# A two-model transformer kernel: the second layer's projection slabs moved into its attention, and TensorE's step reordered

## What is computed

```python
proj = h @ w_in_b[li]
q, k, v, qm = jnp.split(proj, [qw, 2 * qw, 3 * qw], axis=-1)
y_tok = neighbourhood_attn(q.reshape(B, S, N_Q_HEADS, HEAD_DIM),
                           k.reshape(B, S, N_Q_HEADS, HEAD_DIM),
                           v.reshape(B, S, N_Q_HEADS, HEAD_DIM), rpb_b[li])
y_mem = memory_attn(qm.reshape(B, S, N_MEM_HEADS, HEAD_DIM), mk, mv)
x = x + jnp.concatenate([y_tok, y_mem], axis=-1) @ w_out[i]
```

## Time and profile before

| | |
|---|---|
| median of 3 runs | 2664.66 us (2661.65 to 2667.18) |
| profiled execution, its own time | 2679.11 us |
| its span, first to last instruction | 2677.3 us |
| mean granted TensorE clock | 0.967 |
| busy: PE, PEld, DVE, ACT, POOL | 96%, 83%, 36%, 35%, 45% |

### The profile page before, as it was taken

One profiled execution on the slowest core, in us unless ns is written; L12 is line 12 of the kernel. 1 busy time (PEld: TensorE's weight loads), 2 busy tenths in 40 slices (PEclk: granted clock), 3 DMA queues, 4 the chain that ended last, 5 costly groups with the idle time before them and its releaser, 6 DMA issues.

```text
span 2677.3 us, 47067 instructions
## 1 busy us (share of the span) xinstructions
PE 2569.1 (96%) x16758; PEld 2217.9 (83%) x16758; DVE 959.8 (36%) x1740; ACT 923.9 (35%) x2020; POOL 1201.4 (45%) x1039
## 2 busy tenths in 40 slices
PE   7999999999988999999998879999999989999999
PEld 7767888888866888888997769999999767998897
DVE  4263221223255321226753434422433442442341
ACT  4284322232254322234342223222333663322221
POOL 4554444444483444444442534444444442444443
PEclk9999999999988999999998989999999996999999
DMA  5211232232210222232221002222222000222222
GB/s 172 79 42 63 94 101 87 94 100 88 89 42 25 94 97 92 94 103 90 83 74 40 2 25 87 94 95 86 86 95 71 25 25 24 94 91 97 86 100 96
DMA packets 59469, 209.10 MB, mean 78 GB/s; under 512 B 8544, under 2 KB 11232, under 8 KB 59360
## 3 DMA queue, kind: packets, MB, share of 16 engines
q1 hardware_dynamic: 59360, 207.66, 23.1%
HBM read 205.54 MB, written 2.10 MB: 78 GB/s over the span
## 4 chain that ended last, share of the span: by engine, by line
PE 70%; issue 15%; POOL 8%; DVE 4%; ACT 2%; POOLq 0%; DMA 0%; DVEq 0%; SPq 0%; ACTq 0%
PE ps L1307 57%; POOL w_lo L612 7%; PE ps L1495 2%; PE ps L1477 1%; PE ps L1604 1%; PE ps L1454 1%; PE ps L1426 1%; PE ps L1593 1%; DVE s_sb L1784 1%; PE ps L1439 1%; PE ps L1322 1%; PE ps L1500 1%; DVE y_sb L1759 0%; POOL bias_sb L702 0%; PE ps L1504 0%
## 5 line engine op out<-in xcount | busy, mean ns | idle before, releaser
L612 POOL TENSOR_TENSOR w_lo<-raw,w_hi 128x512 fp32r<-128x512 f32 (+1 forms) x704 | 977.2, 1409 | 1164.3 <-ACT w_hi L863 1163.9
L863 ACT ACTIVATE w_hi<-raw 128x512 fp32r<-128x512 f32 (+1 forms) x704 | 427.2, 653 | 1342.2 <-PE ps L1307 1324.7
L1307 PE MATMUL ps<-h_hi,w_hi 128*128 128x512 f32 (+2 forms) x2992 | 854.3, 332 | 14.6 <-POOL h_lo L789 8.0
L1307 PE MATMUL ps<-h_lo,w_hi 128*128 128x512 f32 (+2 forms) x2992 | 852.7, 332 | 0.0
L1307 PE MATMUL ps<-h_hi,w_lo 128*128 128x512 f32 (+2 forms) x2992 | 850.6, 331 | 0.0
L1307 PEld LDWEIGHTS ps<-h_hi,w_hi 128*128 128x128 f32 x2992 | 510.6, 189 | 75.7 <-issue 17.2
L1307 PEld LDWEIGHTS ps<-h_lo,w_hi 128*128 128x128 f32 x2992 | 506.4, 189 | 55.1 <-issue 1.0
L1307 PEld LDWEIGHTS ps<-h_hi,w_lo 128*128 128x128 f32 x2992 | 507.1, 189 | 54.2
L1307 PE MATMUL ps<-act_lo,w_hi 128*128 128x512 f32 (+1 forms) x880 | 280.5, 351 | 0.0
L1307 PE MATMUL ps<-act_hi,w_lo 128*128 128x512 f32 (+1 forms) x880 | 279.8, 350 | 0.0
L1307 PE MATMUL ps<-act_hi,w_hi 128*128 128x512 f32 (+1 forms) x880 | 278.8, 349 | 0.0
(11 more groups left out here) (264 smaller groups left out, 2539.1 us busy)
## 6 DMA issues: line engine op xcount, KB each, us to landing
raw<-slabs_d SPq DMA_DIRECT2D x288, 512.0 KB, 3.2
raw<-slabs_d SPq DMA_DIRECT2D x64, 704.0 KB, 4.0
bias_sb<-alibi_d SPq DMA_DIRECT2D x6, 384.0 KB, 3.7
x<-x_d SPq DMA_DIRECT2D x1, 2048.0 KB, 13.4
out_d<-x SPq DMA_DIRECT2D x8, 256.0 KB, 4.3
rpb_raw<-rpb_d SPq DMA_DIRECT2D x6, 256.0 KB, 2.7
mem_in<-mem_d SPq DMA_DIRECT2D x1, 1024.0 KB, 9.1
cst<-consts_d SPq DMA_DIRECT2D x1, 792.0 KB, 11.2
```

Of the source, the lines that this page charges most:

```text
L612: nc.gpsimd.tensor_tensor(w_lo[:, s, a * P:b * P], raw[:, s, a * P:b * P], w_hi[:, s, a * P:b * P].bitcast(f32), ALU.subtract).then_inc(lo ...
L863: nc.scalar.activation(w_hi[:, s, a * P:b * P], raw[:, s, a * P:b * P], ACT.Copy)\
L1307: last = nc.tensor.matmul(ps[:, s * 2 * BANK + po:s * 2 * BANK + po + n], w[:, s, wk], a[:, k, to:to + n], start=(k == 0 and w is w_hi and ...
```

## The change

The projection keeps 8 slabs ahead of the attention, the 6 of values and the 2 of memory queries. The other 12, now in the order query tile, key tile, query tile and so on, stand inside the attention. Both attentions are one row of 32 pairs, written out without a loop, with the memory heads' 8 pairs first (`woven_row`). TensorE's step is now the transposes of pair p - 2, the scores of p, the values of p - 3, and then half a slab (12 matmuls of 512 columns) in each of the first 24 pairs. In the last 8 pairs stand pieces of the output projection's first two slabs instead, 3 or 6 matmuls each (`OUT_PARTS`), and the rest of these two slabs follows the last pair. ACT's and POOL's steps take a half slab's rounding and remainder each, DVE's odd steps take a slab out. The projected tiles go through a ring of four (`ring`), staged by POOL four pairs ahead of use; scores go through three banks (1, 3 and 5), and both heads' transposes through bank 4, copied out by one ACT instruction instead of two. The attention's results have buffers of their own (`yw_hi`, `yw_lo`), and SP's loads of slabs and of the bias alternate by tile. The number of slabs, pairs and matmuls is the same.

```diff
-    proj(14, 6, 1)
-    out[-1].queries = (0, 1, 2, 6)
-    out[-1].by_cols = True
+    proj(2, 6, 1)
+    out[-1].queries = (0,)
+    out[-1].by_cols = out[-1].woven = True
+    att(nt=2, blocks=m_blocks, bias=None, sink=None, qt=0, kt=0, group=1, y=6, layer=1)
+    out[-1].woven = True
+    slabs(2 * 2, UP)
     att(nt=6, blocks=n_blocks, bias="rpb", sink=None, qt=0, kt=6, group=1, y=0, layer=1)
-    out[-1].by_cols = True
-    att(nt=2, blocks=m_blocks, bias=None, sink=None, qt=12, kt=0, group=1, y=6, layer=1)
-    tail(4, 1, 1, False, (6, 2, True))
+    out[-1].by_cols = out[-1].woven = True
+    slabs(2 * 4, UP)
+    tail(4, 1, 1, False, (6, 2, True), woven=True)
...
+            def attend_woven(a):
+
+                b = stages[stages.index(a) + 1]
+                first, row = a.slab0 // 2, woven_row(a)
+                chores = {a: prepare(a), b: prepare(b)}
+                for s in range(RING):
+                    pool.wait_ge(acc_free[s], first)
+                for n in (0, 1, 2):
+                    chores[a][n](0)
+                stream(a.slab0 + 2)
+                pool.wait_ge(val_kept, a.val0)
+                for p in row:
+                    u, n = p.at // 4, p.at % 4
+                    if p.at + 4 < len(row):
+                        then = row[p.at + 4]
+                        if then.st is b and n < 2:
+                            pool.wait_ge(acc_free[n], first + then.tile + 1)
+                        chores[then.st][n](then.tile)
+                    if n < 2 and 1 <= u <= W_TILES:
+                        split_lo(first + u, 1, UP, (n,))
+                    if n >= 2 and u < W_TILES:
+                        split_lo(first + u + 1, 0, UP, (n - 2,))
+                    if p.back(3).exists:
+                        y_lo_of(p.back(3).st, p.back(3).tile, p.back(3).b)
...
+                if st.woven:
+                    row = woven_row(st)
+                    for p in row:
+                        probs(p, 0)
+                        if p.back(1).exists:
+                            turned_woven(p.back(1))
+                        probs(p, 1)
+                        if p.back(3).exists:
+                            y_hi(p.back(3))
+                        split_woven(p)
...
+                def out_parts(parts):
+                    q = st.slab0 // 2 + W_TILES
+                    near = stages[stages.index(st) + 1]
+                    for s, k in parts:
+                        if k == DT - 2:
+                            begin(q, s)
+                            second_half(q, s)
+                        pe.wait_ge(y_lo_ready, near.pair0 + 4 * (k + 1) if k < near.nt else st.pair0 + 4 * (k - near.nt + 1))
+                        products(q, s, [k], *outputs(st), DT - 2, near.nt - 1)
...
+                if st.woven:
+                    pe.wait_ge(val_kept, st.val0)
+                    row = woven_row(st)
+                    for p in row:
+                        if p.back(2).exists:
+                            transpose(p.back(2))
+                        scores(p)
+                        if p.back(3).exists:
+                            values(p.back(3))
+                        woven_part(p)
+                    last = row[-1]
+                    transpose(last.back(1))
+                    values(last.back(2))
+                    transpose(last)
+                    out_parts([(1, 3)])
+                    values(last.back(1))
+                    values(last)
+                    out_parts([(0, 4), (1, 4), (0, 5), (1, 5)])
+                    return
...
+                def evict_woven(p):
+                    u, n = p.at // 4, p.at % 4
+                    if u >= W_TILES or n % 2 == 0:
+                        return
+                    s, near = n // 2, stages[stages.index(st) + 1]
+                    ended(st.slab0 // 2 + u, s)
+                    if u >= 1:
+                        wait(qk_staged, near.tile0 + u - 1 if u >= 2 else near.tile0)
+                    to = in_cols(ring_tiles(st, u)[s])
+                    stt(to, in_rows(acc(s, 1)), 1.0 if s else HD ** -0.5, in_rows(rstd[:, SEQ_T]), ALU.mult, ALU.mult)\
+                        .then_inc(acc_free[s], 1)
+                if st.woven:
+                    row = woven_row(st)
+                    for p in row:
+                        scores(p)
+                        evict_woven(p)
+                        if p.back(3).exists:
+                            normalise(p.back(3))
```

257 lines of the change are left out of this document (203 added, 54 removed).

## The result

The changed kernel takes 2652.03 us, the median of 7 runs (2647.65 to 2653.77). The kernel before, with four more runs beside it, takes 2677.51 us (7 runs, 2661.65 to 2681.2). The ratio is 0.9913, with a 95% interval of 0.9888 to 0.9938: faster by 0.9%, about 23 us (the medians are 25.5 us apart). Against the median of the three runs shown at first (2664.66) it is 12.6 us.

A forecast was written before the change was run, and what follows sets the result against it. TensorE was taken as the bound, with at most 28.4 us of idle time and low clock to gain. Terms 73.8 + 5.0 + 2.7 + 3.4 + 2.9 + 5.7 = 93.5 against 102.2 us gave 2664.7 - 8.7 = 2656.0, range 2645 to 2672.

The forecast's parts named there:

- the case that had 0.65: Whole kernel: faster by over 0.2% (5.3 us), the forecast and the larger gain taken together, chance 0.65.
- idle at the start: Ahead of the first scores: TensorE waits 4.0 us for query and key staging, then 1.0 us more for POOL, 5.0 us.
- idle for weights in the middle: Half slabs among the pairs: weights are ready about 5.0 us from a turn's start, wanted at 7.4, so no wait.
- idle at pair 24: First output projection piece needs both slab halves; the second is ready 5.0 us into the turn, TensorE there at 2.3: 2.7 us.
- idle at the end: Behind the last values: 1.8 us for tile 5's last result, then 1.6 us for the next slab's first half.
- pairs and slab borders: Attention's 32 pairs: 73.8 us of work, plus 0.09 us for entering a slab in each of 32 turns, 2.9 us.
- clock: Low clock costs 5.7 us: 4.0 in the last 8 turns and what follows, 1.7 at the idle start.
- the slower rival: Half slab at a turn's end, 24 times: weights come too late, kernel over 0.2% slower from 0.6 us excess, chance 0.11.
- The slack of 2.4 us: Middle turns: weights ready after about 5.0 us, TensorE reaches the half slab at 7.4 us, 2.4 us to spare.
- The drain rival: TensorE drains at both borders of each half slab, costing 10.2 us; gain only 1.4 us, 2663, chance 0.07.
- the prediction's 13.6 us for the clock before: Old attention: 102.2 us less 73.8 work and 14.8 idle leaves 13.6, put down to low clock, 44% of 30.7 us.

The follow-up runs named there:

- thin slabs: The changed kernel with only 3 of the 12 slab matmuls in each of the 24 half slabs, the other products left out: 2616.81 us, one run.
- the last version: The changed kernel with earlier query staging, reordered output pieces, a later wait for kept values, and last pieces behind the last values: 2635.97 us, ratio 0.9883.
- the three versions without low time: The changed kernel with earlier query staging (2644.77 us), with reordered output pieces too (2639.35 us), and with kept-values wait and last pieces also moved (2635.97 us).
- the second program: The kernel before with transposes ahead of scores in attentions without slabs, and no slabs inside the second layer's: 2677.52 us, ratio 1.0003.

## Why the prediction was right

I forecast 2656.0 with a range of 2645 to 2672; the kernel takes 2652.0. The time is near partly by luck: I forecast from three runs with a median of 2664.66. From the seven runs' 2677.51 the same gain of 8.7 would have given 2668.8, and for the profiled execution I had 2670.4, where it took 2652.9. Against the seven runs the gain is over 23 us, far more than forecast, and in the profiles what is beyond the second layer's share lies in the last layer, which I had taken for unchanged. It is faster by over 0.2%, the case that had 0.65. For the second layer the mechanism was right. By its own measure, the stretch from the last slab ahead of the attention to the first behind it, the forecast was 171.6 us; it is 673.54 to 842.68, 169.1. (The first half us of it are transposes of values, which before lay outside the stretch.) Less 78.1 for 14 slabs, that is 91.0 us against 93.5 forecast and 102.2 before, a gain of 11.2 instead of 8.7. Term by term:

| term | forecast | measured |
|---|---|---|
| idle at the start | 5.0 | 3.55 + 0.47 = 4.0 |
| idle for weights in the middle | 0 | 0 |
| idle at pair 24 | 2.7 | 3.3 |
| idle at the end | 1.8 + 1.6 | 1.4 + 1.4 |
| pairs and slab borders | 73.8 + 2.9 | 77.1, as the remainder |
| clock | 5.7 | 3.7, an estimate, see below |

**Start.** The chain was right: from DVE's start at 673.58 to the first scores at 677.64 it is 4.1 us, forecast 4.0. But TensorE was not idle from the slab's last matmul on; five transposes of values stood behind it, as they had before, and cover 0.7 us. I had not subtracted them.

**Weights.** The term on which the slower rival stood is right: in 24 turns the half slab waits for POOL only once, 0.47 us in the first, which is the start's. The slack of 2.4 us that I worked out for the chain wasn't measured by itself; with thin slabs it is POOL's load as a whole that binds, once turns are 1.4 us shorter. So what a thinner cover meets first is the rival's engine, but not its chain.

**Pair 24.** Ready 5.2 us into the turn (799.43 to 804.62), forecast 5.0; TensorE gets there at 2.1 us, forecast 2.3. Both misses lengthen the wait.

**Borders.** Pairs and borders together come to 77.1 (91.0 less 10.2 idle and 3.7 clock), forecast 76.7. Turn by turn it is less: turns with 64-row values take 5.42 to 5.47 us, against 2.6 + 2.79 = 5.39, the others 4.95 to 5.03 against 4.92, which is some 2 us over 32 turns. The remainder of 3.3 over 73.8 also holds the transposes at the start and the errors of the other terms. The slab's entry is 0.10 us here (0.34 less 0.24), as the 0.09 of the earlier trace rows. But I took the price from that row alone, and not from the order of forms in a turn, which decides it: with the old order it would have been 4.5 us more. I costed the transposes' new place only for its waits. The drain rival, whose borders cost 10.2 us, would have been about three quarters true there (3.3 + 4.5).

**Clock.** This is the term that was off most. The changed kernel's 10.2 us at 1.2 GHz cost 3.7 us, by an estimate: the last version has the same work, 13.0 us less time, and 9.3 us less idle. TensorE's busy time in the layer says the same: 240.32 us, against 236.46, 236.37 and 236.59 in the three versions without low time. I had foreseen a low spell at the start (6.8 us, forecast 4) and got little of the loss in the tail: 3.4 us low in 43.7 (the window from 799.00), where I had taken 30% of 30 us from the old attention. That the pieces of 3 or 6 matmuls keep the clock up is shown only in small part: without them the low time grew by 3.4 us. With the prediction's 13.6 us for the clock before, the gain of 11.2 is 4.6 idle (14.8 - 10.2) and 9.9 clock (13.6 - 3.7), less 3.3 for the borders (77.1 - 73.8). The 4.6 is measured; the other two are not separate. The 13.6 is what the prices of the pairs left over, 44% of the low time, where the pairs of profiles give 31% (the kernel before, twice: 249.01 - 245.81 us busy for 10.2 us low) to 38%. At these the 30.7 us low cost 9.5 to 11.7, and the clock's share of the gain is 6 to 8 us, which leaves 1.4 us or less for the borders. The runs fix this split to no better than some 2 us.

**What was left out.** The layer gained 13.3 us, of which 2.1 lie outside my stretch. The output projection of before had a low stretch at its start too, at a mean clock of 0.97 in the row of 844.53 above; I had looked at the attention only. And I took the last layer for unchanged. Its 14.4 us in the profile are more than the change's own gain, and without them the two profiles would differ by 12, not by 26. The three runs of before that I forecast from lie in its faster group, which is why 12.6 us against their median agree with the second layer's 13.3.

## What to carry to other kernels

Dense work cut into pieces that stand in every step of a loop that waits on other engines can pay twice, in idle time and in clock, and it must cover each step: here the same work in every second step lost 9 of the 13 us gained, all of it as idle time. Where it joins the loop, put beside it the instructions that use the array in the same form. Then look at the seams, where the pieces begin and end: here they held 10 of 10 us of the layer's idle time left, and mending them took 13.0 us off the layer, as much again as the change itself. And compare many runs, and not two profiles, before a gain in a stage that was not touched is put down to the change.

## What the runs showed of the hardware

- From the start of a slab's last matmul to the start of scores of 64 rows it is 0.33 us, to transposes in the slab's own form 0.24, to another matmul of the slab 0.23 to 0.24. In turns of 5 us that is 0.14 us a turn with what it moves inside the pair.
- Removing 2.4 us of idle time at a stage's start was worth 6.3 us: of two kernels that differ in that edit alone, one profile has 10.2 us low, the other none. Low time cost 31 to 38% of itself, by estimates from pairs of profiles: 3.7 and 3.9 us for 10.2 us low and 3.2 for 10.2 in this layer, 19.6 for 51 in the last.
- The same stretch of instructions, at the same place of two programs that differ only ahead of it, was at 1.2 GHz for 58 us in one and for 6.8 us in the other, worth 19.6 us (274.9 against 255.3); the second program's ten runs, in two groups 17 us apart, say that one program can do both. Its cause stays open. The long stretch was met in two of three profiles without slabs in the second layer and in none of eleven with them.
